# Forget-gate attention scores from queries and keys padded to 128 rows: the bias becomes a row of the product, the causal mask an operand of VectorE

## What is computed

```python
c = jnp.cumsum(logf, axis=-1)
s = einsum('bhqd,bhkd->bhqk', q_i, kf) + c_i[..., :, None] - c[..., None, :]
s = jnp.where(key_pos[None, :] <= q_pos[:, None], s, -jnp.inf)
p = jax.nn.softmax(s, axis=-1)
o = jnp.einsum('bhqk,bhkd->bhqd', p, vf)
```

## Time and profile before

| | |
|---|---|
| median of 3 runs | 1637.7 us (1635.69 to 1638.13) |
| span of the profiled execution, first to last instruction | 1634.2 us |
| own time of the profiled execution | not recorded beside its span |
| TensorE busy | 1578.2 us, 97% of the span |
| VectorE, ScalarE, GpSimd busy | 1005.1 us (62%), 697.6 us (43%), 413.3 us (25%) |
| mean granted TensorE clock | 0.991 of full speed |
| attention stage | about 250 to 348 us of the span |

### The profile page before, as it was taken

How to read it: one execution, slowest core, us unless ns; L and a number is a source line. 1 busy time by engine, 2 the same in 40 slices (tenths; PEclk the granted TensorE clock), 3 DMA queues, 4 the chain that set the end, 5 groups by cost and what they waited for, 6 DMA issues and landing times. The chain is left out here.

```text
span 1634.2 us, 21244 instructions
## 1 busy us (share of the span) xinstructions
PE 1578.2 (97%) x8600; PEld 1326.2 (81%) x8600; DVE 1005.1 (62%) x1444; ACT 697.6 (43%) x1013; POOL 413.3 (25%) x349
## 2 busy tenths in 40 slices
PE   6999998999999999999999999999899999999997
PEld 5778886777888888788888778887688999999886
DVE  7665546557888487433865643346964688886334
ACT  5643345553623343323532334444444644443222
POOL 0024303330722011100042012223542465550002
PEclk9999999999999999999999999999999999999999
DMA  7242222343254254322427422224354122224221
GB/s 298 104 142 91 78 65 94 103 162 145 103 184 177 103 205 172 113 100 81 153 103 268 144 82 94 91 86 142 132 181 164 52 104 104 104 104 155 78 77 52
DMA packets 47068, 203.93 MB, mean 125 GB/s; under 512 B 14352, under 2 KB 14736, under 8 KB 28346
## 3 DMA queue, kind: packets, MB, share of 16 engines
q1 hardware_dynamic: 37346, 171.84, 29.0%
q0 software_dynamic: 9088, 30.38, 5.5%
q10 hardware_dynamic: 536, 0.35, 0.1%
HBM read 181.56 MB, written 21.00 MB: 124 GB/s over the span
## 5 line engine op out<-in xcount | busy, mean ns | idle before, releaser
L559 PE MATMUL ps<-xh,whi 128*128 128x512 f32 (+1 forms) x1136 | 402.9, 355 | 9.7 <-DVE xl L1850 6.9
L561 PE MATMUL ps<-xh,wlo 128*128 128x512 f32 (+1 forms) x1136 | 398.0, 350 | 0.0
L560 PE MATMUL ps<-xl,whi 128*128 128x512 f32 (+1 forms) x1136 | 396.0, 349 | 0.0
L1815 DVE TENSOR_TENSOR wlo<-raw,whi 128x2048 fp32r<-128x2048 f32 x92 | 225.0, 2446 | 143.4 <-ACT whi L1192 143.2
L1192 ACT ACTIVATE whi<-raw 128x512 fp32r<-128x512 f32 (+1 forms) x190 | 236.0, 1246 | 159.0 <-PE ps L561 88.9
L559 PEld LDWEIGHTS ps<-xh,whi 128*128 128x128 f32 x1136 | 215.0, 189 | 49.5 <-issue 20.6
L560 PEld LDWEIGHTS ps<-xl,whi 128*128 128x128 f32 x1136 | 215.9, 190 | 28.5
L561 PEld LDWEIGHTS ps<-xh,wlo 128*128 128x128 f32 x1136 | 214.6, 189 | 29.9
L2240 DVE SCALAR_TENSOR_TENSOR xr<-ps,pc,xr 128x511 f32<-128x511 f32 x88 | 65.2, 746 | 40.0 <-ACT xr L1192 38.5
L2674 POOL TENSOR_TENSOR act<-xr 128x512 f32<-128x512 f32 x22 | 40.0, 1820 | 196.5 <-DVE xr L2240 195.8
L2570 DVE TENSOR_TENSOR wlo<-raw,whi 128x512 fp32r<-128x512 f32 x98 | 79.1, 838 | 0.0
(11 more groups left out here) (457 smaller groups left out, 3507.6 us busy)
## 6 DMA issues: line engine op xcount, KB each, us to landing
raw<-in_w_in SPq DMA_DIRECT2D x35, 1024.0 KB, 5.3
raw<-in_ffn_w SPq DMA_DIRECT2D x33, 1024.0 KB, 4.8
raw<-in_ada SPq DMA_DIRECT2D x24, 1024.0 KB, 4.8
raw<-in_w_up SPq DMA_DIRECT2D x22, 1024.0 KB, 4.9
raw<-in_w_down SPq DMA_DIRECT2D x11, 1024.0 KB, 4.8
xd<-X POOLq DMA_DIRECT2D x8, 512.0 KB, 7.2
td<-vr POOLq DMA_DIRECT2D x16, 256.0 KB, 3.6
raw<-td SPq DMA_DIRECT2D x4, 1024.0 KB, 5.3
```

Of the source, the lines that this page charges most:

```text
L559: pe.e.matmul(o, lh, rh, start=start, stop=False)
L560: pe.e.matmul(o, lh, rl, start=False, stop=False)
L561: return pe.e.matmul(o, ll, rh, start=False, stop=stop)
L1815: up(ve.e.tensor_tensor(lo, raw[conv_at[j] % 3][:, :], hi.bitcast(F32), ALU.subtract), "wlo")
```

## The change

Two pairs of tiles `kz` and `qz` (one for even, one for odd heads) replace `ncb`. The 64 partitions that the head's columns don't use are set to zero, but for one row: ones in `qz`, minus c in `kz`. The score product contracts over all 128 partitions and has the bias in it; the mask matmul is gone. For each head GpSimd loads the row of minus c by a DMA and copies 64 partitions x 512 columns of `qa` and of `ka` into the pair. VectorE's `largest` adds a stretch of a new triangle of 128x512, `tri`, in place of `ncb`; SyncE loads it later. The waits for `ncb` move from VectorE to TensorE, together with one on the copies (`fz`).

```diff
-        ncb = [sb("ncb", [P, S], F32, fs) for _ in range(2)]
+        kz = [sb("kz", [P, S], F32, fs)[:, :] for _ in range(2)]
+        qz = [sb("qz", [P, S], F32, fs)[:, :], qz1]
...
                     b = take(("as", i), "at_s", i + 1)
-                    pe.e.matmul(b[:, 0:n], qa[po_:po_ + 64, ht, P * t:P * t + P], ka[po_:po_ + 64, ht, 0:n],
-                                start=True, stop=False)
-                    done(pe.e.matmul(b[:, P * t:n], ident[:, :], tri[:, :], start=False, stop=True), ("as", i))
+                    pe.wait_ge(sig["fz"], pad_no(hd))
+                    pe.wait_ge(sig[f"ncb{hd % 2}"], 16 * (hd // 2 + 1))
+                    done(pe.e.matmul(b[:, 0:n], qz[hd % 2][:, P * t:P * t + P], kz[hd % 2][:, 0:n], start=True, stop=True),
+                         ("as", i))
...
-                    ve.wait_ge(sig[f"ncb{hd % 2}"], 16 * (hd // 2 + 1))
+                    ve.wait_ge(sig["tri"], 16)
                     ve.wait_ge(sig["at_p"], i - 2)
-                    largest(i, P * (t + 1), sq1[i % 3], ncb[hd % 2][:, 0:P * (t + 1)], st41)
+                    largest(i, P * (t + 1), sq1[i % 3], tri[:, 512 - P * (t + 1):512], st41)
...
-            def fox_bias(hd):
+            def fox_head(hd):
+                o, ht = 64 * (hd % 2), hd // 2
+                r, z = slice(o, o + 64), 64 - o
                 if hd >= 2:
                     po.wait_ge(sig["at_s"], 4 * (hd - 2) + 4)
-                po.e.dma_start(ncb[hd % 2][:, :], bass.AP(ncd.tensor, S * hd, [[0, P], [1, S]])).then_inc(sig[f"ncb{hd % 2}"], 16)
+                po.e.dma_start(kz[hd % 2][z:z + 1, :], ncd[hd:hd + 1, :]).then_inc(sig[f"ncb{hd % 2}"], 16)
+                po.wait_ge(sig["fz"], pad_no(hd - 1))
+                po.wait_ge(sig["rec"], 4 if hd > 2 else 0)
+                copy(qz[hd % 2][r, :], qa[r, ht, :], "fz")
+                copy(kz[hd % 2][r, :], ka[r, ht, :], "fz")
+                po.wait_ge(sig["fz"], pad_no(hd))
 
             po.wait_ge(sig["pe"], at["w", J_V + 1])
-            po.wait_ge(sig["ncd"], 16)
-            fox_bias(0)
...
+            for p in range(2):
+                z = slice(64 - 64 * p, 128 - 64 * p)
+                po.e.memset(kz[p][z, :], 0.0).then_inc(sig["fz"], 1)
+                po.e.memset(qz[p][z, :], 0.0).then_inc(sig["fz"], 1)
+                po.wait_ge(sig["fz"], 3 * p + 2)
+                po.e.memset(qz[p][64 - 64 * p:65 - 64 * p, :], 1.0).then_inc(sig["fz"], 1)
...
-            sp.e.dma_start(tri[:, :], ins["tri"]).then_inc(sig["tri"], 16)
             weights(conv_at[J_V + 1])
             for r in range(4):
                 sp.wait_ge(sig[f"td{r}"], 64)
+            sp.e.dma_start(tri, ins["tri"]).then_inc(sig["tri"], 16)
...
-    c["tri"] = np.where(i[None, :] <= i[:, None], 0.0, -1e30).astype(np.float32)
+    c["tri"] = np.where(np.arange(512)[None, :] <= i[:, None] + 384, 0.0, -1e30).astype(np.float32)
```

More of the change, by code:

```diff
@@ L90 @@
 rt_m hp hz mg_m gr_m f_a xa
-xg xb kpm hd_p hx_p rec act rt_p rt_q zero bias hsum mg_a gr_x
-raw0 raw1 raw2 x0 x1d x2 x3 xsp consts mlp_in taps_in tri rows brow ncb0 ncb1 kd0 kd1 td0 td1 td2 td3 lvm ncd gated ctx tables
+xg xb fz kpm hd_p hx_p rec act rt_p rt_q zero bias hsum mg_a gr_x
+raw0 raw1 raw2 x0 x1d x2 x3 xsp consts mlp_in taps_in tri rows brow ncb0 ncb1 kd0 kd1 td0 td1 td2 td3 ncd gated ctx tables
 tb0 tb1 tb2 tb3 rel0 rel1 vt kk0 kk1 kk2 tq0 tq1 tq2 tq3 tq4 tq5 tq6 hdl0 hdl1 hdl2 hdl3 put
@@ L117, in taps_no, with pad_no @@
     return 10 * n + 4 + 2 * t
+def pad_no(hd):
+    return 6 + 2 * (hd + 1)
 def ada_no(a):
@@ L349, in build @@
         nca = sb("nca", [8, S], F32, m1)
-        row = sb("row", [1, D], F32, m1)
-        tri = sb("tri", [P, P], F32, m1)
+        rowb = sb("row", [P, D], F32, m1)
+        row, tri, qz1 = rowb[0:1, :], rowb[:, 0:512], rowb[:, 512:1024]
         acc2, acc2_r = twins("acc2", [P, 2048], m1)
@@ L803, in tiles_of @@
                 return [o[:, t, P * k:P * k + P] for t in range(4)]
-            pe.wait_ge(sig["tri"], 16)
-            pe.wait_ge(sig["qa"], 4)
-            pe.wait_ge(sig["ka"], 4)
             pe.wait_ge(sig["va"], 4)
@@ L830, in tensor_program @@
                     hd, t = divmod(i, 4)
-                    ht, po_, n = hd // 2, 64 * (hd % 2), P * (t + 1)
+                    n = P * (t + 1)
                     b = take(("as", i), "at_s", i + 1)
-                    pe.e.matmul(b[:, 0:n], qa[po_:po_ + 64, ht, P * t:P * t + P], ka[po_:po_ + 64, ht, 0:n],
-                                start=True, stop=False)
-                    done(pe.e.matmul(b[:, P * t:n], ident[:, :], tri[:, :], start=False, stop=True), ("as", i))
+                    pe.wait_ge(sig["fz"], pad_no(hd))
+                    pe.wait_ge(sig[f"ncb{hd % 2}"], 16 * (hd // 2 + 1))
+                    done(pe.e.matmul(b[:, 0:n], qz[hd % 2][:, P * t:P * t + P], kz[hd % 2][:, 0:n], start=True, stop=True),
+                         ("as", i))
                     if 11 <= i <= 14:
@@ L2051, in levels @@
                 if 0 <= s < 14:
-                    ve.wait_ge(sig["lvm"], 16)
+                    ve.wait_ge(sig["ncd"], 32)
                     for hf in range(2):
@@ L2707, in spectrum @@
                 po.e.dma_start(kd[i // 2, 4 * (i % 2) + 2 + f], b).then_inc(sig[f"kd{u % 2}"], 16)
-            po.e.dma_start(lvm[:, :, :], ins["levels"]).then_inc(sig["lvm"], 16)
+            po.e.dma_start(lvm[:, :, :], ins["levels"]).then_inc(sig["ncd"], 16)
             def taps_out(n, t):
@@ L2751, in gpsimd_program, with copy @@
                     taps_out(1, 3)
-            def fox_bias(hd):
+            def copy(dst, src, signal):
+                po.e.tensor_copy(dst, src).then_inc(sig[signal], 1)
+            def fox_head(hd):
+                o, ht = 64 * (hd % 2), hd // 2
+                r, z = slice(o, o + 64), 64 - o
                 if hd >= 2:
                     po.wait_ge(sig["at_s"], 4 * (hd - 2) + 4)
-                po.e.dma_start(ncb[hd % 2][:, :], bass.AP(ncd.tensor, S * hd, [[0, P], [1, S]])).then_inc(sig[f"ncb{hd % 2}"], 16)
-            po.wait_ge(sig["pe"], at["w", J_V + 1])
-            po.wait_ge(sig["ncd"], 16)
-            fox_bias(0)
-            fox_bias(1)
-            fox_bias(2)
+                po.e.dma_start(kz[hd % 2][z:z + 1, :], ncd[hd:hd + 1, :]).then_inc(sig[f"ncb{hd % 2}"], 16)
[4 more added lines that the diff above has]
+                po.wait_ge(sig["fz"], pad_no(hd))
+            po.wait_ge(sig["pe"], at["w", J_V + 1])
+            po.wait_ge(sig["tp"], taps_no(1, 3))
+            for p in range(2):
[4 more added lines that the diff above has]
+                po.e.memset(qz[p][64 - 64 * p:65 - 64 * p, :], 1.0).then_inc(sig["fz"], 1)
+            po.wait_ge(sig["ncd"], 32)
+            po.wait_ge(sig["qa"], 4)
+            po.wait_ge(sig["ka"], 4)
+            fox_head(0)
+            fox_head(1)
+            fox_head(2)
             spectrum(0)
@@ L2769, in gpsimd_program @@
             for hd in range(3, 8):
-                fox_bias(hd)
+                fox_head(hd)
                 spectrum(hd - 2)
```

## The result

| | before | after |
|---|---|---|
| median | 1637.91 us (1635.69 to 1638.25, 4 runs) | 1628.82 us (1627.78 to 1631.25, 4 runs) |
| ratio, 95% interval | | 0.9947 [0.9934, 0.9959] |
| run again later, with more runs | 1637.90 us (17 runs) | 1628.65 us (6 runs), 0.9941 [0.9922, 0.9960] |
| span of the profiled execution | 1634.2 us | 1627.0 us (its own time 1628.78) |
| TensorE busy, instructions | 1578.2 us, 8600 | 1563.1 us, 8536 |

The change is 9.1 us faster by the medians and 7.2 us by the spans. The forecast was 6.7 us. It started from 1637.7 us, the median of the first three runs of before.

What follows compares the result with a forecast made beforehand. TensorE, busy nearly throughout, was taken as the bound where the stage waits for nothing else. Terms -0.8 - 6.9 + 1.0 = -6.7 us took 1637.7 to 1631.0 us; the mechanism's own range was 1628.0 to 1635.5, the wider one 1627.0 to 1637.5.

Steps and rivals of the forecast that it cites:

- Part (a): Steps 0 to 8, where ScalarE and VectorE set the time: TensorE's saving turns idle, 0 gained up to 269.65.
- The step's saving: Each score step on TensorE: mask 0.24 us plus gaps of 0.18 after and 0.07 ahead, 0.49 in all.
- The gaps stay: Rival: a step saves only the mask's 0.24 us; 3.2 us gained, 1634.5 us; chance 0.07.
- Part (b): Steps 9 to 12: a 3.8 us wait for GpSimd's copies partly replaces the wait for `mx`; 0.8 us gained.
- bound of +2.3: Upper bound on the gain in steps 9 to 12, in us; the lower bound was -2.3.
- The clock: After the longer pause before step 12, 2 us more at 1.2 GHz, costing 1.0 us, between 0 and 2.5.
- Slower, by the clock: Rival: longer pause and extra idle time keep TensorE at 1.2 GHz through steps 13 to 26; 1642.5 us; chance 0.10.
- Part (c): Steps 13 to 26, TensorE without a pause: fourteen scores at 0.49 us, 6.9 us gained if others keep up.
- The gain goes to VectorE: Rival: GpSimd's copies slow the low parts of steps 11 and 19; 1.3 us gained, 1636.4 us; chance 0.13.
- Three signs: Expected in the trace: no TensorE pause in steps 13 to 26, step 11's low part 3.5 to 6 us, copies 0.7 to 1.3.
- GpSimd: Its work per head in steps 13 to 26: 6.8 us against TensorE's 8.8, so it keeps up.
- Part (d): From `largest` of step 26 to `head_scale`: VectorE and ScalarE's 13.5 us chain doesn't shrink; step 31's pause grows to about 3.7.

Runs made afterwards that it cites:

- first group, mask_0_8_27_31: Changed kernel with the mask matmul back in steps 0 to 8 and 27 to 31: 1628.03 us, ratio 0.9940.
- both moves: Changed kernel with head 3's DMA and copies behind the first gate product and `w_o`'s high and low parts in steps 22 and 23: 1627.87 and 1627.41 us.
- w_o_step_23: Changed kernel with the high and low parts of `w_o` made in steps 22 and 23 in place of 26 and 27: 1630.57 us, ratio 0.9959.

## Why the prediction held, and where its terms were off

The direction, the mechanism and the division into parts held; the time came 2.2 us below the 1631.0 forecast, inside its range. That it came so near owes something to luck: several terms were off, and some cancelled. Point by point:

- **Part (a), 0 gained: right.** The mask can be put back there at no price (first group), and the bank for step 8's L565 still comes from ScalarE, at 269.53 (269.65). The pause ahead of it grew from 0.19 to 1.11 us: TensorE's saving became idle time.
- **The step's saving, 0.49: mis-sized.** It is 0.61. The mask's 0.24 held (0.23 measured alone), the gap ahead was 0.09 in place of 0.07, and the gap behind was taken as 0.42 - 0.24 = 0.18. The row it was compared with, the mask's, was itself lengthened by the 64-row neighbour (0.24 against 0.14 behind a padded score). The padded score costs 0.15 to the next row, so the gap was 0.27. "The gaps stay" is dead: 64-row scores without a mask cost 0.39 us a step., read as the reason for the gaps, was read too strongly, as its idle 0.76 us stands behind a product of 512 columns; the loads of step 16 show the same thing at 128 columns.
- **Part (b), 0.8 gained: the parts right, the sum helped by errors that cancel.** TensorE is ready for step 12 at 278.29 (forecast 278.2: four steps at 0.49 stand for three at 0.61, as step 8's score lies ahead of 269.65), and the forecast pause of 3.8 us is 4.02. The copy beside VectorE's low part was stretched from 0.62 to 2.12 us, so that two copies at a forecast 2.0 took 2.7. The assumption that copies disturb the low part by half was wrong: it is the copy that pays, and the low part ended at 281.2 where the forecast had 283.5, by the bound for an undisturbed low part (281.4). The sum has a slip too: half way between 281.4 and 286.5 is 284.0 and not 283.5, which would leave 0.3 us of gain. The bound of +2.3 doesn't follow either, since TensorE's own 283.9 allows 1.1. The gather went at 285.64, which is 0.6 later than before and not 0.8 earlier. That is because the clock fell ahead of step 12, not behind it, and the same low stretch of 6.8 us was over 3 us earlier. So at step 16 TensorE is well ahead.
- **The clock, +1.0: not in the stage.** The fall at step 12 has the same length, 6.8 us, in both profiles. It costs about 3.0 us in the kernel after and, by the same reckoning, 17.96 - 2.50 - (9.40 + 4 x 0.61) = 3.6 in before, so -0.6 in place of +1.0. The gain up to step 16 was therefore 3.3 us against 1.3: 4 x 0.61 = 2.4 of product (steps 12 to 15, where the forecast counted step 12 apart), and 0.9 of part (b) and the clock together. What the rival "Slower, by the clock" feared didn't come: behind 289 the clock is full until 332. The fall of 3.4 us there meets the prediction's sign against itself (a clock below 1 behind 292) to the letter, but before has one like it at 346 to 350.
- **Part (c), 14 x 0.49 = 6.9, no pause: two errors that cancel.** From step 16's score to `largest` of step 26 it is 27.52 us before and 22.49 after, 5.0 gained. Eleven steps (16 to 26) at the forecast 0.49 are 5.4, at the measured 0.61 6.7; head 5's pauses of 1.6 us took the difference. Of the rival "The gain goes to VectorE" the mechanism is true in this one place, though no copy causes it: the low part takes 2.98 us, beside the end of an addition, as it took 2.92 in before. The steps have become short enough to feel it. Three signs were missed here and in part (b): no pause in steps 13 to 26, a low part of 3.5 to 6 us in step 11 (3.45), and copies of 0.7 to 1.3 us (0.62 alone, 2.12 beside the low part).
- **GpSimd: right.** A head's additions, DMAs and copies take 5.7 us (301.34 to 307.04) where 6.8 were forecast. Heads 4 to 7 wait for no copy, even when each is made twice.
- **Part (d), a fixed chain of 13.5: right.** 13.54 us. The pause for it grew to 2.79 us, and step 30 has two new ones of 0.46 and 0.27 us (for ScalarE's `pt` and VectorE's `kr`); together 3.5, where 3.7 was forecast for one. Taking the low part out of the chain shortens it to 11.32.
- **From span to median.** The forecast kept 3.5 us between them. The kernel after has 1.8 in both of its profiles (1628.78 - 1627.0, 1629.01 - 1627.2). By that the profiled execution of before took some 1636.0 us (an estimate), 1.7 to 1.9 below its median. That is most of what separates 7.2 us of span from 9.1 us of median: the spans understate the gain, and both pairs of medians give 9.1 to 9.3. Among 66 runs of before in the experiments the fastest is 1630.69 and the slowest 1641.56.

What stays open: how the 9.1 us of the medians divide between the stage (8.3 in the profiles) and the clock behind it, why the stage's 3.0 us of both moves give about 1 in the median, and why the runs of the `w_o` move fall in two groups. The profiles point to where the clock falls behind the stage, but no run here moves such a fall without moving something else.

## What to carry to other kernels

In this kernel a float32 matmul of 64 rows among full-height ones costs more than a padded one of the same columns: its price is read as the difference of two whole steps, and not against a neighbour's row, which it may lengthen too. When work is taken from TensorE, look next at what the other engines do once per head or per stage (a long low part, a late copy behind a product), for that is where the shortened steps first stop. And put what a waiting matmul needs ahead of long work in its producer's queue, but count on the gain only when the wait behind it is known. When positions in two profiles are compared, look first whether the clock fell alike in both.

## What was not expected of the hardware

- A product of 64 rows lengthens the row behind it too: the mask before L559 takes 0.24 us there, and 0.14 behind a padded score. In all the height costs 0.39 us a step at 2.4 GHz, at 128 and at 512 columns alike (steps of 1.86 and 3.06 us, 1.47 and 2.66 padded).
- Who pays for GpSimd and VectorE side by side hangs on GpSimd's operation. A two-input addition stretches VectorE's low part (5.24 us and 3.45 against 2.28). A one-input copy of 64x512 is itself stretched, from 0.62 to 2.12 us, and ends 0.5 us behind the low part; in the run with 64-row scores the low part beside such a copy alone takes 2.29 us. The order of starting doesn't decide it: the low part starts first both beside the addition of before (279.07 and 279.64) and beside the copy in the rows below. The Trainium skill (GPSIMD Engine Reference, "Specifications") names the contention; that the copy is the one that waits is what these rows show:

```profile
278.97 2.29 DVE L1820 TENSOR_TENSOR Xr<-raw,Xr 128x2048 fp32r<-128x2048 f32 x1 [0.36 <-ACT Xr L1197]
```

```profile
279.46 2.28 POOL L2760 COPY row<-qa 64x512 f32<-64x512 f32 x1
```

- A fall of the clock costs by where it lies. The one at step 12 was 6.8 us long with a pause of 2.50, of 4.02 and of 5.71 us, cost 3.6, 3.0 and 1.8 us, and was cheapest where the pause covered most of it. The pause's length doesn't foretell it either. With a pause of 4.0 us it lasted 6.8 us in three profiles and 3.4 in two (`mask_0_8_27_31` and `w_o_step_23`). With 64-row scores and a pause of 2.31 us there was none at step 12. With head 3's copies early and no pause over 1.2 us there were 3.4 us, and the kernel with both moves had none there in one profile and 3.4 us in the other.
